# Products of two mixers and of the norms' sums, issued between a weight piece's two halves instead of behind the piece

## The reference

```python
# first_block
proj = rmsnorm(h, g) @ w_in                    # 2048 x 10240
ya = dilated_mixture_attention(qa, ka, va)     # 12 heads in three groups, softmax over all groups' keys
yb = stick_breaking_attention(qb, kb, vb)      # 4 heads, cumulative sums of log(1 - beta)
mix = (sigmoid(gla) * (ya @ w_branch_a) + sigmoid(glb) * (yb @ w_branch_b)) @ w_out
h = h + rmsnorm(mix, g)
h = h + rmsnorm((gelu(gate) * value) @ w_down, g)          # gate, value = conv(u @ w_up)
h = h + sigmoid(h @ w_ple_gate) * (p @ w_ple_in)
# second_block
proj = rms_norm(x, g) @ w_in_2 + b_in_2        # 2048 x 5888
attn = sliding_window_attention(q, k, v, sinks)            # 16 heads of 64
y = s5_ssm(u, ...)                                         # 32 groups of 64 complex states
# gated branches, w_out_2, then a second feed-forward block and a last norm
```

## Time and profile before

| | us |
|---|---|
| median of 3 runs | 2671.74 (2670.56 to 2674.57) |
| span of the profiled execution | 2672.7 |
| PE busy | 2642.9 (99%) |
| DVE busy | 1804.4 (68%) |
| ACT busy | 1274.7 (48%) |
| POOL busy | 249.9 (9%) |
| mean granted clock of PE | 0.995 |
| stage `mix`, about 208.8 to 441.2 | 232.4, PE busy 232.4, DVE 124.3, ACT 121.0 |
| stage `in2`, about 1458.7 to 1741.5 | 282.8, PE busy 279.1, DVE 253.5, ACT 163.9 |

### The profile page before, as it was taken

The page is one execution under the profiler, slowest core; times in us unless marked ns, Lnnn a source line. Parts: engine busy times, 40 slices in busy tenths (PEclk is TensorE's granted clock), DMA queues, the critical chain, the costliest instruction groups (busy, mean ns, idle before and its releaser), DMA issues.

```text
span 2672.7 us, 57540 instructions
## 1 busy us (share of the span) xinstructions
PE 2642.9 (99%) x22834; PEld 2628.9 (98%) x22834; DVE 1804.4 (68%) x2269; ACT 1274.7 (48%) x1548; POOL 249.9 (9%) x206
## 2 busy tenths in 40 slices
PE   9999999999999999999999999999999999999998
PEld 9999999999999999999999999999999999999998
DVE  5455555747888888864467999867576777775444
ACT  5334455345344444444455556554455555554442
POOL 1000000030000000001101665400100000000000
PEclk9999999999999999999999999999999999999999
DMA  7665556574555655556656555556656666666664
GB/s 256 193 199 175 150 161 182 169 213 148 173 195 196 196 194 189 196 191 203 192 168 200 174 163 157 155 183 200 194 183 195 196 194 193 191 190 197 195 191 141
DMA packets 137806, 496.71 MB, mean 186 GB/s; under 512 B 15425, under 2 KB 15425, under 8 KB 137537
## 3 DMA queue, kind: packets, MB, share of 16 engines
q1 hardware_dynamic: 137520, 494.20, 59.7%
q10 hardware_dynamic: 144, 0.52, 0.1%
HBM read 492.57 MB, written 2.10 MB: 185 GB/s over the span
## 4 chain that ended last, share of the span: by engine, by line
PE 89%; DVE 6%; DVEq 2%; ACT 1%; DMA 1%; issue 1%; ACTq 0%; SPq 0%
PE bank L432 86%; DVE w_lo L982 2%; PE ps_a L432 1%; PE ps_o L432 1%; PE ps_n L432 1%; DVE act_lo L1021 1%; PE ps_t L432 0%; DMA hT<-in_xT 0%; ACT w_hi L676 0%; DMA w_raw<-in_w_in 0%; ACT act_hi L742 0%; DVE hT L1046 0%; DVE pr L1309 0%; DVE rstd L1005 0%; DVEq L1299 0%
## 5 line engine op out<-in xcount | busy, mean ns | idle before, releaser
L982 DVE TENSOR_TENSOR w_lo<-w_raw,w_hi 128x1024 fp32r<-128x1024 f32 x928 | 1134.1, 1234 | 720.8 <-ACT w_hi L676 719.2
L676 ACT ACTIVATE w_hi<-w_raw 128x1024 fp32r<-128x1024 f32 x928 | 977.0, 1056 | 1185.9 <-PE bank L432 1045.3
L432 PE MATMUL bank<-act_hi,w_hi 128*128 128x256 f32 x5408 | 1275.3, 279 | 3.0 <-DVE gate_y L1350 2.5
L432 PE MATMUL bank<-act_lo,w_hi 128*128 128x256 f32 x5408 | 1264.9, 277 | 0.0
L432 PEld LDWEIGHTS bank<-act_hi,w_hi 128*128 128x128 f32 x5408 | 1014.9, 188 | 4.1 <-issue 2.7
L432 PEld LDWEIGHTS bank<-act_lo,w_hi 128*128 128x128 f32 x5408 | 1015.7, 188 | 0.7
L432 PE MATMUL bank<-act_hi,w_lo 128*128 128x256 f32 x5408 | 726.9, 277 | 2.7 <-DVE w_lo L982 2.7
L432 PEld LDWEIGHTS bank<-act_hi,w_lo 128*128 128x128 f32 x5408 | 666.6, 188 | 3.1 <-DVE w_lo L982 3.1
L432 PE MATMUL bank<-f_lo,w_hi 128*128 128x256 f32 x1408 | 327.9, 276 | 0.0
L432 PE MATMUL bank<-f_hi,w_hi 128*128 128x256 f32 x1408 | 327.9, 276 | 0.0
L432 PEld LDWEIGHTS bank<-f_lo,w_hi 128*128 128x128 f32 x1408 | 264.3, 188 | 0.0
(11 more groups left out here) (227 smaller groups left out, 1790.3 us busy)
## 6 DMA issues: line engine op xcount, KB each, us to landing
w_raw<-in_w_up SPq DMA_DIRECT2D x352, 512.0 KB, 4.2
w_raw<-in_w_in SPq DMA_DIRECT2D x252, 512.0 KB, 4.2
w_raw<-in_w_down SPq DMA_DIRECT2D x176, 512.0 KB, 4.2
w_raw<-in_w_out SPq DMA_DIRECT2D x64, 512.0 KB, 4.4
w_raw<-in_w_ple_gate SPq DMA_DIRECT2D x32, 512.0 KB, 4.5
w_raw<-in_w_branch_attn SPq DMA_DIRECT2D x16, 512.0 KB, 3.9
w_raw<-in_w_branch_a SPq DMA_DIRECT2D x8, 512.0 KB, 4.1
w_raw<-in_w_branch_b SPq DMA_DIRECT2D x8, 512.0 KB, 3.5
```

Source lines behind the costliest of these rows:

```text
L432: return pe.matmul(o, l, r, start=start, stop=stop, skip_group_check=True)
L676: act.activation(w_hi[:, k, 0:n, :], w_raw[:, k, 0:n, :], ACT.Copy).then_inc(hi_ready, 1)
L982: dve.tensor_tensor(w_lo[:, k, 0:n, :], w_raw[:, k, 0:n, :], w_hi[:, k, 0:n, :].bitcast(F32), ALU.subtract).then_inc(lo_ready, 1)
```

## The change

The call of `beside` in the general branch moves from behind the low products to between the high products and the wait for `lo_ready`. The number of products, the DMAs and the other engines' programs stay as they are. Since `piece_used` is counted by the last low product, it is now counted behind the mixer's products of the same piece, where it was counted ahead of them.

```diff
                                 w = w_hi[:, k, t, c * P:(c + 1) * P]
                                 mm(o, w, xh[:, x, :], j == 0 and t == 0 and c == 0, False)
                                 mm(o, w, xl[:, x, :], False, False)
+                        if isinstance(i, int) and beside:
+                            beside(i * st.ppb + at)
                         pe.wait_ge(lo_ready, q + 1)
                         for t in range(n):
                             x = x0 + j * PIECE_KT + t
                             for c in range(2):
                                 last = mm(ps[:, c * TOK:(c + 1) * TOK], w_lo[:, k, t, c * P:(c + 1) * P],
                                           xh[:, x, :], False, j == st.pieces[s] - 1 and t == n - 1)
                         last.then_inc(piece_used, 1)
-                        if isinstance(i, int) and beside:
-                            beside(i * st.ppb + at)
                 bodies(pe, st, body)
```

## The result

The changed kernel takes 2689.15 us in the median (2688.14 to 2693.28, 4 runs), beside 2672.78 us (2670.56 to 2674.57, 4 runs) of the kernel before on the same chip: a ratio of 1.0065, 95% interval 1.0054 to 1.0077. It is 16.4 us slower. The forecast was 2691 us. That forecast was reckoned from 2671.7 us for the kernel before, so it was a rise of 19.3 us.

A forecast was written before the change was run, and what follows sets the result against it. PE's products plus its waits were taken to bound the kernel. Terms 15.8 + 2.1 + 0.9 = 18.8 us, 19.5 with releases, took the 2672.7 us span to 2692, forecast as 2691 us; range 2678 to 2700.

The forecast's parts named there:

- PE stands in the wait: On PE, low products behind a waiting mixer product cannot pass it; each microsecond of waiting counts as one of time.
- Even units, 1.6 us each: `mix`, units 0, 2, 4, 6: PE waits for ACT's copy behind an exponential needing DVE's later maximum; 6.4 us together.
- Odd units 0.9, unit 7 and transposes 0.5: `mix`: units 1, 3, 5 wait 0.9 us each for the copy, 2.7 together; unit 7's copy and transposes 0.5 together.
- Second attention, 2.6 + 3.6 us: `mix`, four heads: waits for softplus at the cumulative sums, 2.6 us, and for ACT's weights at the value products, 3.6.
- Mix in sum: All waits forecast in `mix`: 6.4 + 2.7 + 0.5 + 2.6 + 3.6 = 15.8 us.
- Spacing, taken at nothing: Weight products behind a mixer start 0.118 instead of 0.113 us apart; no change assumed, bounds 8 us either way.
- Rival C: Faster: slow spacing behind mixers ends sooner, up to 8 us come back; 2664 us without waits, chance 0.05.
- `in2`, 2.1 us: Stage `in2`: 0.9 us once in the DVE-bound stretch, and 1.2 us for copy waits at pieces 44, 56 and 68.
- Norm's sum in stage `in`, 0.9 us: Stage `in`: the squares' sum starts no earlier and the low products come behind it, 0.9 us; other four sums nothing.
- A: Only the shift by the low products counts, the later `piece_used` lengthens no chain: 8 us, 2680 us, chance 0.15.
- B: Waits of 1.6 us or longer drop PE's clock, 4 x 1.6 to 2 us on top: 2698 us, chance 0.17.
- D: Nothing: gains in spacing and waits cancel, or PE's queue lets low products pass; 2672 us, chance 0.06.

The follow-up runs named there:

- seventh-eighth placement: Changed kernel with the mixer put between the seventh and eighth of a piece's low products; 2677.18 us, ratio 1.0018 to the kernel before.
- copy-first kernel: Changed kernel with ACT's copy of the turned probabilities put ahead of the next unit's exponential; 2680.7 us, ratio 1.0030 to the kernel before.
- ACT's earlier release: Changed kernel with ACT's rounding in `mix` and `in2` released by the last high product, DVE's subtraction still by `piece_used`; 2674.3 us, ratio 1.0006.
- the control: Kernel before, old order kept, with only ACT's rounding in `mix` and `in2` released by the last high product; 2671.76 us, ratio 1.0000.

## Why the prediction was right

**What bounds the kernel.** PE's products and waits, right: all that came is PE's idle time, and no other engine's busy time moved by more than 3 us.

**PE stands in the wait.** Right: in the changed kernel the low products begin at 256.96, behind the mixer from 256.27, with their weights long ready. The rule that the forecast cited, of the Trainium skill, page "TensorE: Matmul & The Clock Gate", section "The mechanism" (matmuls start in program order), agrees with this.

**Even units, 1.6 us each.** Right: 1.55 by the brackets, and by experiment in its two parts. The seventh-eighth placement left 0.78 for the later `piece_used`, and in the copy-first kernel the even units did not wait at all, as no chain through the maximum was left.

**Odd units 0.9, unit 7 and transposes 0.5.** They waited 0.82 each (8.8 - 4 x 1.55 - 0.15, over 3), 0.15 and 0.22 us. Right, a little too high.

**Second attention, 2.6 + 3.6 us: the mis-sized term.** Heads 0 and 2 waited as forecast, 0.87 on `sp_b` and 1.0 on `t_b`. Heads 1 and 3 did not wait at all. Head 1 in the changed kernel, PE, then DVE's softplus and ACT's weights:

```profile
388.72 1.07 PE L432 MATMUL bank<-act_hi,w_lo 128*128 128x256 f32 x8
...
396.88 1.04 PE L432 MATMUL ps_t<-sp_b,tab 128*128 128x256 f32 x6
```

```profile
403.32 0.89 PE L432 MATMUL ps_o<-t_b,proj 128*128 128x256 f32 x4
```

```profile
395.45 0.55 DVE L1093 SCALAR_TENSOR_TENSOR sp_b<-z_b,l_b 128x384 f32<-128x384 f32 x1
```

```profile
402.73 0.51 ACT L823 ACTIVATE t_b<-lw_b 128x384 f32<-128x384 f32 x1
```

Both operands are in time, by 0.88 and 0.08 us. The step that failed is "For head 1 ... the chain is 10.51", counted from the piece of the head's scores. The softplus is ready at 396.00, which is 6.38 us after piece 50's low products end (388.72 + 0.90). In the kernel before, piece 50 ended at 372.81 + 1.22 (mixer) + 2.91 = 376.94, and the softplus was ready at 383.32, again 6.38 us later. So for this head the ring released ACT by piece 50, not by piece 49, and the new order brought that release nearer by the mixer of piece 49. The weights of head 1 are the same case. Their last rounding waited for PE, in the kernel before and in the changed one:

```profile
389.16 1.06 ACT L676 ACTIVATE w_hi<-w_raw 128x1024 fp32r<-128x1024 f32 x1 [2.65 <-PE bank L432]
```

```profile
401.76 1.06 ACT L676 ACTIVATE w_hi<-w_raw 128x1024 fp32r<-128x1024 f32 x1 [1.74 <-PE bank L432]
```

The low products of piece 54 end at 388.89 and 401.50, and the weights are ready 1.74 us later both times, so piece 54 released them and not piece 53, from which I had counted 5.44 us. In all I counted 2 x 0.43 + 2 x 0.8 = 2.5 us too much.

**Mix in sum.** The brackets add up to 8.8 + 2.0 + 1.7 + 0.2 = 12.7 us in 13 waits. Starting and stopping adds 13 x 0.28 = 3.6, which the brackets hide. The closer spacing gives back 2.2: 910 places at 0.118 us are 423, each worth 0.0046 us. That makes 14.1, measured 14.2, forecast 15.8. My terms for these same waits come to 15.8 - 2.5 = 13.3 us, and they cost 12.7 + 3.6 = 16.3, so I had 3.0 us too little there. The 2.5 for heads 1 and 3 and the 2.2 of the spacing err the other way. That the sum of `mix` is only 1.6 us off is in part luck.

**Spacing, taken at nothing.** Wrong, to the good: a gain of 1.8 to 2.2 us in `mix` (up to 8 was the bound). Rival C had the place and the sign right and the size wrong: the slow stretch behind a mixer is some 24 products where it is there, not 8, and with every wait gone 1.8 us come back, not 8.

**`in2`, 2.1 us, measured 3.0.** The DVE-bound stretch cost 1.1 us (forecast 0.9): its first wait grew to 2.73 us, more than the 2.3 forecast, but the wait for the turned state at 1550.01 in the kernel before, 1.3 us, was gone, because the clock had fallen (15 starts at 0.21 us, 1.5 us in all) and PE came later. With ACT's earlier release the first wait was 2.4 us, the clock did not fall there, the second wait stayed at 1.3, and the stage was still 1.0 us longer than before. That DVE's instants do not depend on PE there holds only nearly: the earlier release shortened the first wait by 0.3 us here, and from 1.4 to 1.0 us in the control. Of the four waits in that stretch the profile puts only the first down to DVE, the others to ACT's operands. The three places at pieces 44, 56 and 68 cost 0.57, 0.56 and 0.83 us, where I had 0.4 each: their brackets are 0.38, 0.38 and 0.65, and the difference is mostly the restart.

**Norm's sum in stage `in`, 0.9 us.** PE waited 0.86 for POOL, 1.1 with the restart. The stage took 208.1 to 208.8 us in four traces with the old order there and 209.3 to 210.1 in five with the new one.

**Sum.** By stages 14.2 + 3.0 + 1.2 = 18.4 us, against 19.5 forecast and 16.4 between the medians; the chance variation outside the two stages is as large as what is left. The time of 2689.15 us lies 1.9 us from the 2691, but the rise is overrated by 2.9 us; the kernel before came out 1.0 us higher in these runs, and that hides 1.0 of it.

**Rivals.** A (only the shift) is refuted by the 1.55 us waits and by the 0.78 left without the shift. B (the clock falls behind waits of 1.6 us) did not happen in `mix` of the changed kernel; with the mixer amid the high products the clock did fall there, behind waits of 1.8 us and more, and in `in2` behind 2.73. D is out by the intervals.

## What to carry to other kernels

A step that waits for another engine is not moved ahead of work that engine's release depends on without counting both effects: PE comes earlier by what it is moved past, and the release comes later by the step itself. Here the margins of the copies were 0.1 to 0.2 us, and moves of 0.11, 0.92 and 1.83 us, each with the later `piece_used`, cost 5, 16 and 56 us. If such a move is wanted, release each buffer at its last reader, and put the operation that the waiting engine needs next ahead of the one that it needs later. And read each head's or tile's chain by itself: the release that decides can be another piece's for every second one.

## What was not expected of the hardware

- The clock does not follow from the length of the idle time alone. PE's longest wait for `w_lo` is 2.09 us in the kernel before and in the changed one. There the eight products behind it took 1.80 us, here 1.21:

```profile
1395.26 1.21 PE L432 MATMUL bank<-act_hi,w_lo 128*128 128x256 f32 x8 [2.09 <-DVE w_lo L982]
```

  In the kernel with the mixer amid the high products a wait of 1.80 us was followed by slow products (eight in 1.53 us) and one of 1.81 us, 36 us later, was not (1.09 us):

```profile
276.42 2.01 PE L432 MATMUL ps_o<-pT_buf,proj 128*128 128x128 f32 x12 [1.80 <-ACT pT_buf L807]
279.93 1.53 PE L432 MATMUL bank<-act_hi,w_lo 128*128 128x256 f32 x8
...
312.05 1.61 PE L432 MATMUL ps_o<-pT_buf,proj 128*128 128x128 f32 x12 [1.81 <-ACT pT_buf L807]
...
314.43 1.09 PE L432 MATMUL bank<-act_hi,w_lo 128*128 128x256 f32 x8
```

  Nor does the place decide. In each of the eleven traces PE waits 2.45 to 2.47 us once for DVE's `gate_y` (line 1350). In eight of them 12 or more weight products behind it begin 0.2 us or more apart; in three, the control among them, they don't, and the granted clock of the 3 us from that wait on is 0.50 in the kernel before and 1.00 in the control.

  None of the 1.55 us waits did it. In the changed kernel's `in2` the wait of 2.73 us did: products begin 0.21 us apart, the 1.2 GHz level, 15 of them:

```profile
1553.55 0.92 PE L432 MATMUL ps_t<-kpad,proj 128*128 128x128 f32 x4 [2.73 <-DVE s_buf L1267]
1554.12 1.68 PE L432 MATMUL bank<-act_hi,w_lo 128*128 128x256 f32 x8
1555.59 0.41 PE L432 MATMUL bank<-act_hi,w_hi 128*128 128x256 f32 x1
1555.80 0.41 PE L432 MATMUL bank<-act_lo,w_hi 128*128 128x256 f32 x1
```

- The spacing of 0.118 instead of 0.113 us holds for some 40 weight products behind a mixer that stands behind the piece, and for some 24 behind one that stands ahead of the low products. In both cases it ends at low products, those of the second piece behind the mixer and those of the next piece. It does not follow every mixer. In the kernel before 19 of the 29 mixer groups in `mix` have the 40. In the changed kernel 16 of 29 have the 24 or nearly, and the others next to none. Of the 13 groups for which PE had to stop 9 are without it (unit 0's among them: 2.82 us from 256.96 to 259.78, against 2.91 from 248.91 to 251.82), and of the 16 others 4 are. What makes it was not tried and stays open.
